# Alternating halves of the matmul array: 64-row score products and 64-wide value products in pairs

## The chip, the core and the metric

The kernel runs on one core of one Trainium2 chip. TensorE does the matmuls, VectorE, ScalarE and GpSimd the rest, and the queue on SyncE starts every load. The metric is the device time of one execution in microseconds, shown as the median of the runs.

## What is computed

One layer of a decoder in float32, 256 tokens of width 1024: a combined input projection, two attention branches of 8 heads each, gates, an output projection, and a sparse expert network (top 4 of 32 experts). Cut to the parts that matter here:

```
z = h @ W_in
A: multi-head latent attention: s = q_nope.k_nope + q_rot.k_rot (64 + 32 wide), causal softmax, p @ v (a v of 64 for each head)
B: sparse attention: index scores relu(q_idx . k_idx) of 8 heads, 64 wide, weighted and summed, top 64 keys of each query;
   s = q . k (64 wide, one k for all heads), softmax over the chosen keys, p @ v (one v of 64 for all heads)
x = x + W_out(sigmoid(g_A) * (A @ W_bA) + sigmoid(g_B) * (B @ W_bB))
x = x + experts(x), 12 MB of float32 weights for each of the 32 experts
```

## The kernel before

All work is written out by hand for each engine, with semaphores between the engines; an engine runs its instructions in the order of the code. The program has a front (everything up to the router) and a stage of 32 expert items. The expert weights come in units of 2 MB into a ring of twelve slots; a slot is loaded again when TensorE has read it (semaphore `used`).

Tokens are two tiles `t` of 128. A query tile t = 0 sees 128 keys, t = 1 sees 256. `BATCHES` lists six batches of head products that fill one PSUM bank of 512 columns: four heads for t = 0, two heads for t = 1. It is used three times:

- **index stage**: `scores` (L568) for b = 0 to 5 with the index q and k, in banks `SB[0]` and `SB[1]` in turn; ScalarE takes the relu of each batch (L987), VectorE adds it to the scores. One block of the gate projection (`gate_block`, L526, 8 matmuls of 256 columns) stands behind b = 3. Then `turn_pairs` transposes the q of branch B (L530).
- **attention loop**, iterations b = 0 to 11 on TensorE: scores of batch b + 1 (`scores_of`), values of batch b - 1 (`values`, L705), a gate block (b = 0 to 10), and the four transposes of the probabilities of batch b (`turn_probs`, L530). Batches 0 to 5 are branch A (96 rows), 6 to 11 branch B (`kT`, `qT`, 64 rows).
- For each batch VectorE masks the scores and finds the row maximum (`masked(b + 1)`), ScalarE takes the exponentials, VectorE divides by the sum (`normalised(b)`) and goes on with a piece of the top-k search for branch B; ScalarE copies the transposed probabilities to `probT` (L1051), which `values(b)` waits for (semaphore `pT_ok`).

The operands decide which part of the 128 x 128 array a matmul uses. In branch B and in the index stage head h has its 64 rows of q and k in partitions 0 to 63 (h even) or 64 to 127 (h odd), so its score product takes the upper or the lower half of the rows. A value product has 64 columns, and its output goes to partitions 0 to 63 (h even) or 64 to 127 (h odd), the left or the right half of the columns. The batches of before hold heads of one parity each, so the products of a batch all use the same half. A float32 matmul of the program is two rows "MATMUL" in the trace, called passes below.

The loop of TensorE before:

```python
            for b in range(12):
                if b < 11:
                    scores_of(b + 1)
                if b:
                    values(b - 1)
                if b in GATES_ATT:
                    gate_block()
                turn_probs(b)
```

Of the kernel before, what the change touches and what calls it, by code (L numbers as in the profile page):

```python
# [14 lines left out]
P = 128  # L15
# [42 lines left out]
BATCHES = [(0, (0, 2, 4, 6)), (0, (1, 3, 5, 7)),  # L58
           (1, (0, 2)), (1, (1, 3)), (1, (4, 6)), (1, (5, 7))]
# [5 lines left out]
GATES_IDX = (3,)  # L65
# [24 lines left out]
def build(nc, x, positions, attn_norm_g, w_in, mla_q_norm_g, mla_w_uq, mla_kv_norm_g, mla_w_ukv,  # L90
# [4 lines left out]
    with ctx:  # L95
# [106 lines left out]
        TURN = TB + SB  # L202
        ACC, GU, PREP, DN = B[0:4], B[4:6], B[6], B[7]
# [319 lines left out]
        def _(pe):  # L523
# [40 lines left out]
            def scores(b, q, k, signal):  # L564
                t, heads = BATCHES[b % 6]
                w = P * (t + 1)
                for m, h in enumerate(heads):
                    mm = pe.matmul(SB[b % 2][:, m * w:(m + 1) * w], q(h, t), k(h, w), start=True, stop=True)  # L568
                mm.then_inc(signal, 1)

            def pair_q(h, t):
                return qT[HD * (h % 2):HD * (h % 2) + HD, h // 2, t * P:(t + 1) * P]

            def pair_k(h, w):
                return kT[HD * (h % 2):HD * (h % 2) + HD, 0:w]
# [103 lines left out]
            def scores_of(b):  # L679
                if b >= 2:  # L680
                    pe.wait_ge(s_mx, b - 1)
                if b < 6:
                    scores(b, lambda h, t: qmT[:, h, t * P:(t + 1) * P], lambda h, w: kmT[:, h, 0:w], s_ps)
                else:
                    scores(b, pair_q, pair_k, s_ps)

            def turn_probs(b):
# [3 lines left out]
                for m in range(4):  # L691
                    tr = turned(TB[b % 2][:, m * P:(m + 1) * P], prob[:, b % 2, m * P:(m + 1) * P])
                tr.then_inc(pT_ps, 1)

            def values(b):
                t, heads = BATCHES[b % 6]
                pe.wait_ge(pT_ok, b + 1)
                if b in (6, 8):
                    pe.wait_ge(pv_ok, t + 1)
                for m in range(4):  # L700
                    h = heads[m // (t + 1)]
                    kt = m % (t + 1)
                    half = V_DIM * (h % 2)
                    v = v_ml[:, kt, h, :] if b < 6 else z_kv[:, kt, HD:2 * HD]
                    mm = pe.matmul(VB[t][half:half + V_DIM, (h // 2) * P:(h // 2 + 1) * P], v,  # L705
# [846 lines left out]
```

## Time and profile before

| | |
|---|---|
| median of 3 runs | 1149.29 us (1148.4 to 1149.75) |
| time of the profiled execution | 1149.92 us |
| its span, first to last instruction | 1148.1 us |
| mean granted TensorE clock | 0.993 of full speed |
| HBM read | 429.92 MB |

The time is 1.8 us more than the span of the same execution, and the profiled execution is 0.6 us above the median.

### The profile page before, as it was taken

The numbers are of one execution on the slowest core, as the hardware profiler recorded it, in microseconds if no ns is written. First come the engines' busy times: TensorE is split into PE (matmuls) and PEld (weight loads), VectorE is DVE, ScalarE is ACT, GpSimd is POOL, SyncE is SP. The second block draws the span as 40 slices with busy tenths as digits, with TensorE's granted clock in tenths as the row PEclk, the third lists the DMA queues.
The fourth block names the chain that finished last, engine by engine and source line by source line (L and its number), as shares of the span: only waits on it lengthen the run. The fifth ranks groups of instructions, "written<-read, shape, count | busy, mean of one in ns | idle before, by whom it ended". The sixth has DMA issues, their size and how long they took to land.

```text
span 1148.1 us, 13190 instructions
## 1 busy us (share of the span) xinstructions
PE 1100.0 (96%) x5094; PEld 478.2 (42%) x5094; DVE 279.3 (24%) x663; ACT 164.0 (14%) x341; POOL 10.2 (1%) x28
## 2 busy tenths in 40 slices
PE   7999999999999999999999999999999999999996
PEld 5578878553333333333333333333333333333332
DVE  2056533121222222222222222211111111112223
ACT  2144431211111010000011001000000000000002
POOL 0101000000000000000000000000000000000000
PEclk9999999998999999999999999999999999999999
DMA  9823541968999999999999999999999999999994
GB/s 316 324 74 147 220 200 56 369 263 350 432 432 430 431 432 433 430 430 432 432 432 430 430 432 433 430 431 431 433 432 430 430 433 433 430 431 432 433 431 196
DMA packets 43411, 431.23 MB, mean 376 GB/s; under 512 B 5825, under 2 KB 8257, under 8 KB 18785
## 3 DMA queue, kind: packets, MB, share of 16 engines
q1 hardware_dynamic: 43392, 430.99, 89.3%
q8 instruction: 12, 0.20, 0.1%
q14 instruction: 7, 0.05, 0.0%
HBM read 429.92 MB, written 1.05 MB: 375 GB/s over the span
## 4 chain that ended last, share of the span: by engine, by line
PE 65%; DMA 22%; SPq 10%; issue 1%; DVE 1%; ACT 1%; another core or an unknown queue 0%; DVEq 0%; ACTq 0%
PE bank L865 24%; DMA raw<-in_w_gate_up 21%; PE bank L881 12%; PE bank L526 8%; SPq L436 7%; PE bank L530 5%; PE bank L559 4%; PE bank L804 3%; SPq L439 3%; PE bank L837 3%; PE bank L751 2%; PE bank L568 1%; PE bank L705 1%; PE bank L769 1%; DMA x_res<-in_x 0%
## 5 line engine op out<-in xcount | busy, mean ns | idle before, releaser
L865 PE MATMUL bank<-raw,xT 128*64 128x512 f32 x2048 | 463.9, 599 | 27.3 <-DMA raw<-in_w_gate_up 25.9
L865 PEld LDWEIGHTS bank<-raw,xT 128*64 128x64 f32 x2048 | 140.1, 137 | 322.8 <-issue 258.3
L881 PE MATMUL bank<-raw,actT 128*64 128x512 f32 x1024 | 232.3, 595 | 0.0
L1440 DVE COPY ev_gu<-bank 128x512 f32<-128x512 f32 x32 | 22.1, 692 | 499.8 <-PE bank L865 499.8
L881 PEld LDWEIGHTS bank<-raw,actT 128*64 128x64 f32 x1024 | 70.8, 137 | 131.8 <-issue 124.7
L1433 DVE TENSOR_TENSOR gub<-bank,bias_gu 128x512 f32<-128x512 f32 x64 | 43.9, 686 | 169.5 <-PE bank L530 169.5
L1100 ACT COPY ev_gu<-bank 128x512 f32<-128x512 f32 x32 | 18.8, 586 | 392.7 <-PE bank L865 392.7
L837 PE MATMUL bank<-ev,gated 64*128 64x512 f32 x256 | 63.6, 615 | 1.2 <-ACT ev L1110 0.8
L804 PE MATMUL bank<-x_res,onehot 128*64 128x512 f32 x264 | 62.3, 592 | 0.0
L526 PE MATMUL bank<-hT,front_raw 128*128 128x256 f32 x256 | 58.9, 383 | 0.0
L526 PEld LDWEIGHTS bank<-hT,front_raw 128*128 128x128 f32 x256 | 47.5, 190 | 8.4 <-issue 2.5
L559 PE MATMUL bank<-front_raw,hT 128*128 128x512 f32 (+2 forms) x128 | 47.0, 531 | 1.1 <-DVE hT L1172 1.1
L530 PEld LDWEIGHTS bank<-cst,ev_gu 128*128 128x128 f32 x256 | 33.4, 210 | 25.9 <-issue 25.9
L1105 ACT ACTIVATE ev_gu<-gub 128x512 f32<-128x512 f32 x32 | 20.2, 630 | 154.7 <-DVE gub L1442 154.7
L530 PE MATMUL bank<-cst,ev_gu 128*128 128x128 f32 x256 | 39.7, 298 | 0.0
L837 PEld LDWEIGHTS bank<-ev,gated 64*128 64x128 f32 x256 | 22.1, 186 | 41.7 <-issue 41.0
L804 PEld LDWEIGHTS bank<-x_res,onehot 128*64 128x64 f32 x264 | 18.9, 137 | 37.2 <-issue 37.1
L559 PEld LDWEIGHTS bank<-front_raw,hT 128*128 128x128 f32 x128 | 25.7, 207 | 20.6 <-issue 20.5
L1110 ACT COPY ev<-bank 128x512 f32<-128x512 f32 x32 | 18.8, 586 | 82.9 <-PE bank L881 82.9
L1084 ACT COPY ev<-bank 128x512 f32<-128x512 f32 x33 | 19.3, 586 | 66.5 <-PE bank L804 66.5
L1093 ACT COPY gated<-bank 128x256 f32<-128x256 f32 x32 | 11.9, 372 | 113.4 <-PE bank L530 113.4
L1456 DVE TENSOR_TENSOR actT<-gub,ev_gu 128x512 f32<-128x512 f32 x32 | 22.2, 693 | 24.4 <-PE bank L881 24.3
(235 smaller groups left out, 599.5 us busy)
## 6 DMA issues: line engine op xcount, KB each, us to landing
raw<-in_w_gate_up SPq DMA_DIRECT2D x128, 2048.0 KB, 43.0
raw<-in_w_down SPq DMA_DIRECT2D x64, 2048.0 KB, 45.9
front_raw<-in_w_in SPq DMA_DIRECT2D x6, 2048.0 KB, 12.9
front_raw<-in_w_out SPq DMA_DIRECT2D x2, 2048.0 KB, 9.6
front_raw<-in_w_branch_mla SPq DMA_DIRECT2D x1, 2048.0 KB, 7.7
front_raw<-in_w_branch_dsa SPq DMA_DIRECT2D x1, 2048.0 KB, 7.7
front_raw<-in_w_in SPq DMA_DIRECT2D x1, 1664.0 KB, 16.3
x_res<-in_x SPq DMA_DIRECT2D x2, 512.0 KB, 4.4
```

What stands on the lines that cost most here:

```text
L436: sp.dma_start(raw[:, slot, :], w_gu_v[e, u // 2, :, u % 2 * UNIT:(u % 2 + 1) * UNIT]).then_inc(raw_in[slot], 16)
L439: sp.dma_start(raw[:, slot, :], w_dn_v[e, u]).then_inc(raw_in[slot], 16)
L526: mm = pe.matmul(o, lhs(c), rhs(c), start=start and c == 0, stop=c == n - 1)
L530: return pe.transpose(o, src, ident)
L559: mm = pe.matmul(ZB[t][:, 0:w], hT[:, c, t * P:(t + 1) * P], unit3(n, w)[:, c, :], start=c == 0, stop=c == KC - 1)
L751: mm = pe.matmul(B[2 * t + n][:, :], mT[:, c, t * P:(t + 1) * P], unit3(U_WO + n)[:, c, :], start=c == 0, stop=c == KC - 1)
L804: mm = pe.matmul(PREP[half * SLOTS:(half + 1) * SLOTS, :], onehot[:, t, :], xs[:, t, half * BLK:(half + 1) * BLK], start=t == 0, stop=t == ...
L837: mm = pe.matmul(ACC[2 * t + half][:, :], scat[rows, t * P:(t + 1) * P], ev[rows, :], start=False, stop=True, skip_group_check=True)
L865: mm = pe.matmul(GU[pair][half * SLOTS:(half + 1) * SLOTS, :], xT[:, c, b, :], w[:, at:at + BLK], start=u == 0 and k == 0, stop=last and k ...
L881: mm = pe.matmul(DN[half * SLOTS:(half + 1) * SLOTS, :], actT[:, c, u, :], w[:, at:at + BLK], start=u == 0 and c == 0, stop=u == DN_UNITS ...
L1433: dve.tensor_tensor(gub[:, pair, :].rearrange("p (j s) -> p j s", s=SLOTS), GU[pair][:, :].rearrange("p (j s) -> p j s", s=SLOTS), bias_gu ...
L1456: dve.tensor_tensor(actT[:, :, :, :].rearrange("p c h s -> p (c h s)"), lin, sig, ALU.mult).then_inc(act_ok, 1)
```

## The change

`BATCHES` now pairs the heads as (0, 1, 2, 3), (4, 5, 6, 7) and (0, 1), (2, 3), (4, 5), (6, 7), and is used for branch A alone, where the values of a batch now alternate between the column halves. `PAIR_BATCHES` is the old list, and serves the index stage and branch B. There two batches, one of even and one of odd heads, are issued together: `pair_scores` alternates between the row halves and writes two banks, `pair_values` multiplies the one v with all heads of a batch in one matmul (512 or 2 x 256 columns) and alternates between the column halves. VectorE and ScalarE do the same work as before; in the index stage batches 2 and 3 lie in other banks. The core of the diff:

```diff
-BATCHES = [(0, (0, 2, 4, 6)), (0, (1, 3, 5, 7)),
-           (1, (0, 2)), (1, (1, 3)), (1, (4, 6)), (1, (5, 7))]
+BATCHES = [(0, (0, 1, 2, 3)), (0, (4, 5, 6, 7)),
+           (1, (0, 1)), (1, (2, 3)), (1, (4, 5)), (1, (6, 7))]
+PAIR_BATCHES = [(0, (0, 2, 4, 6)), (0, (1, 3, 5, 7)),
+                (1, (0, 2)), (1, (1, 3)), (1, (4, 6)), (1, (5, 7))]
-GATES_IDX = (3,)
+GATES_IDX = (2,)
+        IDX_BANKS = (SB, TB, SB)
+            def pair_scores(b, banks, signal):
+                t = PAIR_BATCHES[b][0]
+                w, n = P * (t + 1), len(PAIR_BATCHES[b][1])
+                for m in range(n):
+                    for k in range(2):
+                        h = PAIR_BATCHES[b + k][1][m]
+                        rows = slice(HD * k, HD * k + HD)
+                        mm = pe.matmul(banks[k][:, m * w:(m + 1) * w], qT[rows, h // 2, t * P:(t + 1) * P], kT[rows, 0:w],
+                                       start=True, stop=True)
+                        if m == n - 1:
+                            mm.then_inc(signal, 1)
-            for b in range(6):
-                if b >= 2:
-                    pe.wait_ge(idx_rl, b - 1)
-                scores(b, pair_q, pair_k, idx_ps)
+            for b in range(0, 6, 2):
+                if b == 4:
+                    pe.wait_ge(idx_rl, 2)
+                pair_scores(b, IDX_BANKS[b // 2], idx_ps)
                 if b in GATES_IDX:
                     gate_block()
             pe.wait_ge(qb_rot, 1)
+            pe.wait_ge(idx_rl, 4)
             turn_pairs(z_qb, qd_ps)
...
                 else:
-                    scores(b, pair_q, pair_k, s_ps)
+                    pe.wait_ge(s_mx, b)
+                    pair_scores(b - 6, SB, s_ps)
...
+            def pair_values(b):
+                t, heads = PAIR_BATCHES[b - 6]
+                pe.wait_ge(pT_ok, b + 2)
+                pe.wait_ge(pv_ok, t + 1)
+                n = len(heads) * P
+                at = (heads[0] // 2) * P
+                for kt in range(t + 1):
+                    for k in range(2):
+                        mm = pe.matmul(VB[t][V_DIM * k:V_DIM * (k + 1), at:at + n], z_kv[:, kt, HD:2 * HD],
+                                       probT[:, (b + k) % 2, kt * n:(kt + 1) * n], start=kt == 0, stop=kt == t)
+                        if kt == t:
+                            mm.then_inc(pv_ps, 1)
...
-                if b < 11:
+                if b < 6 or b in (7, 9):
                     scores_of(b + 1)
-                if b:
+                if 0 < b < 7:
                     values(b - 1)
+                elif b in (8, 10):
+                    pair_values(b - 2)
...
-            values(11)
+            pair_values(10)
```

TensorE in the index stage, from the first index scores to the transposes of the next q (banks 4 and 5 are `SB`, 2 and 3 are `TB`, L526/L531 is the gate block, xN counts matmuls). Before:

```order
L568 MATMUL bank4<-kT,qT 128x128 x4
L568 MATMUL bank5<-kT,qT 128x128 x4
L568 MATMUL bank4<-kT,qT 128x256 x2
L568 MATMUL bank5<-kT,qT 128x256 x2
L526 MATMUL bank0<-hT,front_raw 128x256 x8
L568 MATMUL bank4<-kT,qT 128x256 x2
L568 MATMUL bank5<-kT,qT 128x256 x2
L530 MATMUL bank2<-cst,z_qb 128x128 x4
```

And of the change, the end of the same stretch, from the last scores of 128 columns on:

```order
L585 MATMUL bank5<-kT,qT 128x128
L585 MATMUL bank2<-kT,qT 128x256
...
L585 MATMUL bank3<-kT,qT 128x256
L531 MATMUL bank0<-hT,front_raw 128x256 x8
L585 MATMUL bank4<-kT,qT 128x256
L585 MATMUL bank5<-kT,qT 128x256
```

The matmuls are as many as before, but two of one bank no longer follow each other, and batches 2 and 3 stand in banks that no relu of batches 0 and 1 has to free.

TensorE in branch B, iterations 7 and 8 of the attention loop (`area_p` is `prob` or `probT`, `sq` holds v). Before:

```order
L568 MATMUL bank4<-kT,qT 128x256 [waits s_mx]
L568 MATMUL bank4<-kT,qT 128x256
L705 MATMUL bank6<-area_p,sq 64x128 [waits pv_ok,pT_ok]
L705 MATMUL bank6<-area_p,sq 64x128 x3
L526 MATMUL bank0<-hT,front_raw 128x256 [waits g_ok,raw_in2]
L526 MATMUL bank0<-hT,front_raw 128x256 x7
L530 MATMUL bank3<-cst,area_p 128x128 [waits pT_ok,p_ok]
L530 MATMUL bank3<-cst,area_p 128x128 x3
L568 MATMUL bank5<-kT,qT 128x256 [waits s_mx]
L568 MATMUL bank5<-kT,qT 128x256
L705 MATMUL bank6<-area_p,sq 64x128 [waits pT_ok]
```

And in the change:

```order
L585 MATMUL bank<-kT,qT 128x256 [waits s_mx]
L585 MATMUL bank<-kT,qT 128x256 x3
L531 MATMUL bank<-hT,front_raw 128x256 [waits g_ok,raw_in2]
L531 MATMUL bank<-hT,front_raw 128x256 x7
L535 MATMUL bank<-cst,area_p 128x128 [waits pT_ok,p_ok]
L535 MATMUL bank<-cst,area_p 128x128 x3
L731 MATMUL bank<-area_p,sq 64x512 [waits pv_ok,pT_ok]
L731 MATMUL bank<-area_p,sq 64x512
```

Scores of two batches stand together in the odd iterations, values of two batches in the even ones, where they now come straight behind the transposes that their `pT_ok` rests on; before, scores stood between the two.

## Rows read from the trace of the kernel before

**Rows 1.** Stretches: busy us of each engine with instructions, TensorE clock, DMA share, GB/s

```profile
240.00:245.00 5.00, 4.31 (x26) 2.37 (x26) 1.14 (x3) 0.59 (x1) 0.00 (x0) 1.00 0.00 0
...
270.00:275.00 5.00, 5.00 (x26) 1.85 (x24) 0.00 (x0) 0.00 (x0) 0.00 (x0) 1.00 0.58 190
280.00:690.00 410.00, 410.00 (x1942) 148.41 (x1940) 89.51 (x185) 43.21 (x78) 0.00 (x0) 1.00 1.01 431
690.00:1148.00 458.00, 421.53 (x1954) 146.36 (x1950) 95.73 (x200) 47.42 (x87) 0.00 (x0) 0.99 0.97 417
```

**Rows 2.** Timeline of TensorE, index stage: start, us, passes (x), idle before

```profile
61.94 3.52 PE L568 MATMUL bank<-kT,qT 64*128 64x128 f32 x24
65.39 3.72 PE L526 MATMUL bank<-hT,front_raw 128*128 128x256 f32 x16
69.04 1.14 PE L568 MATMUL bank<-kT,qT 64*128 64x256 f32 x8
70.11 1.09 PE L530 MATMUL bank<-cst,z_qb 128*128 128x128 f32 x8
```

**Rows 3.** Timeline of ScalarE, relu of index batch 3

```profile
66.85 0.60 ACT L987 ACTIVATE area_p<-bank 128x512 f32<-128x512 f32 x1 [0.95 <-DVE score L1221]
```

**Rows 4.** Timeline of TensorE, values in branch A

```profile
105.75 1.09 PE L705 MATMUL bank<-area_p,v_ml 128*64 128x128 f32 x8
106.77 3.72 PE L526 MATMUL bank<-hT,front_raw 128*128 128x256 f32 x16
```

**Rows 5.** Timeline of VectorE and TensorE, up to `turn_probs(3)`

```profile
100.00 0.69 DVE L1300 SCALAR_TENSOR_TENSOR area_p<-bank,cst 128x512 f32<-128x512 f32 x1 [1.27 <-PE bank L568]
...
121.25 0.69 DVE L1311 TENSOR_TENSOR area_p<-area_p,den 128x512 f32<-128x512 f32 x1
...
122.27 0.60 PE L530 MATMUL bank<-cst,area_p 128*128 128x128 f32 x4
```

**Rows 6.** Timeline of TensorE, branch B, iterations 6 and 7

```profile
134.43 0.60 PE L530 MATMUL bank<-cst,area_p 128*128 128x128 f32 x4
...
137.06 3.72 PE L526 MATMUL bank<-hT,front_raw 128*128 128x256 f32 x16
140.62 0.60 PE L530 MATMUL bank<-cst,area_p 128*128 128x128 f32 x4
141.15 1.13 PE L568 MATMUL bank<-kT,qT 64*128 64x256 f32 x4
142.21 1.09 PE L705 MATMUL bank<-area_p,sq 128*64 128x128 f32 x8
143.22 3.72 PE L526 MATMUL bank<-hT,front_raw 128*128 128x256 f32 x16
```

**Rows 7.** Timeline of VectorE, branch B, iteration 7

```profile
142.31 0.69 DVE L1295 SCALAR_TENSOR_TENSOR area_p<-bank,allow 128x512 f32<-128x512 f32 x1 [3.74 <-PE bank L568]
```

**Rows 8.** Timeline of TensorE, iteration 11 and the end of the loop

```profile
165.27 0.60 PE L530 MATMUL bank<-cst,area_p 128*128 128x128 f32 x4
166.54 1.09 PE L705 MATMUL bank<-area_p,sq 128*64 128x128 f32 x8 [0.67 <-ACT area_p L1051]
167.56 0.66 PE L530 MATMUL bank<-cst,area_p 128*128 128x128 f32 x4
168.05 1.89 PE L526 MATMUL bank<-mlaT,front_raw 128*128 128x256 f32 x8
```

**Rows 9.** Timeline of TensorE, expert stage: products alternating between column halves

```profile
282.89 3.62 PE L881 MATMUL bank<-raw,actT 128*64 128x512 f32 x16
286.43 1.23 PE L530 MATMUL bank<-cst,ev_gu 128*128 128x128 f32 x8
```

**Rows 10.** Stretch of the lower TensorE clock, columns as in Rows 1

```profile
262.60:269.50 6.90, 5.47 (x18) 2.44 (x18) 4.59 (x9) 0.63 (x1) 0.00 (x0) 0.51 0.72 306
```

**Rows 11.** Timeline of TensorE, gate and up products of expert items 0 and 1

```profile
242.51 13.95 PE L865 MATMUL bank<-raw,xT 128*64 128x512 f32 x64
...
265.50 15.86 PE L865 MATMUL bank<-raw,xT 128*64 128x512 f32 x64 [1.43 <-DVE xT L1424]
```

More of the change, by code:

```diff
@@ L562, in z_unit, with scores @@
                     z_n += 1
-            def scores(b, q, k, signal):
-                t, heads = BATCHES[b % 6]
+            def scores(b):
+                t, heads = BATCHES[b]
                 w = P * (t + 1)
                 for m, h in enumerate(heads):
[L568 to L575, printed above, removed]
+                    mm = pe.matmul(SB[b % 2][:, m * w:(m + 1) * w], qmT[:, h, t * P:(t + 1) * P], kmT[:, h, 0:w],
+                                   start=True, stop=True)
+                mm.then_inc(s_ps, 1)
+            def pair_scores(b, banks, signal):
[6 more added lines that the diff above has]
+                        mm = pe.matmul(banks[k][:, m * w:(m + 1) * w], qT[rows, h // 2, t * P:(t + 1) * P], kT[rows, 0:w],
+                                       start=True, stop=True)
+                        if m == n - 1:
+                            mm.then_inc(signal, 1)
             def turn_pairs(zq, signal):
@@ L682, in scores_of @@
                 if b < 6:
-                    scores(b, lambda h, t: qmT[:, h, t * P:(t + 1) * P], lambda h, w: kmT[:, h, 0:w], s_ps)
+                    scores(b)
                 else:
-                    scores(b, pair_q, pair_k, s_ps)
+                    pe.wait_ge(s_mx, b)
+                    pair_scores(b - 6, SB, s_ps)
             def turn_probs(b):
@@ L691, in turn_probs @@
                 for m in range(4):
-                    tr = turned(TB[b % 2][:, m * P:(m + 1) * P], prob[:, b % 2, m * P:(m + 1) * P])
+                    at = (m % 2) * 2 + m // 2 if b >= 8 else m
+                    tr = turned(TB[b % 2][:, at * P:(at + 1) * P], prob[:, b % 2, m * P:(m + 1) * P])
                 tr.then_inc(pT_ps, 1)
             def values(b):
-                t, heads = BATCHES[b % 6]
+                t, heads = BATCHES[b]
                 pe.wait_ge(pT_ok, b + 1)
[L698 to L705, printed above, removed]
-                                   probT[:, b % 2, m * P:(m + 1) * P], start=kt == 0, stop=kt == t)
-                mm.then_inc(pv_ps, 1)
+                for kt in range(t + 1):
+                    for n, h in enumerate(heads):
+                        m = n * (t + 1) + kt
+                        half = V_DIM * (h % 2)
+                        mm = pe.matmul(VB[t][half:half + V_DIM, (h // 2) * P:(h // 2 + 1) * P], v_ml[:, kt, h, :],
+                                       probT[:, b % 2, m * P:(m + 1) * P], start=kt == 0, stop=kt == t)
+                mm.then_inc(pv_ps, 1)
+            def pair_values(b):
[4 more added lines that the diff above has]
+                at = (heads[0] // 2) * P
+                for kt in range(t + 1):
+                    for k in range(2):
[3 more added lines that the diff above has]
+                            mm.then_inc(pv_ps, 1)
             pe.wait_ge(up_d, 4)
@@ L1212, in _ @@
             for b in range(6):
-                t, heads = BATCHES[b]
+                t, heads = PAIR_BATCHES[b]
                 w = P * (t + 1)
```

10 lines of the change are left out of this document (5 added, 5 removed).

## The prediction

> **What bounds the kernel now.** I read the stretches first, to learn which part of the program a gain can come out of. The program has two regimes. In the middle and late part the DMA engines are full: share 1.01 at 431 GB/s from 280 us on [rows 1], with TensorE busy all 410 us up to 690, and 421.53 of 458 us after that, when it waits for weights. So in the expert stage the weight stream sets the pace in the end. But the stream does not start by itself. It stands still at 240 to 245 us (DMA share 0.00) and is at 0.58 at 270 to 275 us [rows 1], because all twelve slots of the ring are full and only TensorE's reading frees one. From about 273 us on it never stops again. The end is therefore that moment plus the bytes that are left: what TensorE saves before its first expert products moves the whole stream, and with it the end, one to one. What it would save after 280 us would be worth nothing, and the change touches nothing there.
>
> Then the front, by the timeline of TensorE. In branch B the rows follow each other without an idle time [rows 6], and VectorE idles 3.74 us there for the next scores [rows 7]: TensorE is the bound. The one exception is in branch A. VectorE starts the first mask at 100.00 us and has, with its pieces of the top-k search, next to no gap until the division of batch 3 ends at 121.25 + 0.69 = 121.94 us; `turn_probs(3)` comes at 122.27 [rows 5]. There TensorE is only 0.33 us behind the point where VectorE would hold it.
>
> **What a pass costs.** The gate block: 16 passes of 256 columns from 137.06 to 140.62, 0.22 us each with the change of shape [rows 6]; so about 0.108 us for 128 columns, 0.43 for 512. The values of before: 8 passes of 128 columns, all in one column half, from 105.75 to 106.77 [rows 4]: 1.02 us, that is 8 x 0.108 and 0.15 for the change of shape. Half an array is no faster than a whole one, if only one half is used.
>
> **Do the halves run side by side?** For the row halves the trace already shows it. Index batches 4 and 5, one even and one odd, wait for nothing between them: 8 passes of 256 columns from 69.04 to 70.11 [rows 2], 1.07 us. A single batch of 4 such passes takes 1.06 us (141.15 to 142.21) [rows 6]. Two batches at the price of one. For the column halves the trace shows it at 512 columns: the down products alternate, and 16 passes take 282.89 to 286.43 [rows 9], 3.54 us or 0.22 a pass, where one half alone would need 0.43. At 128 and 256 columns it isn't shown. Its bounds are nothing gained (8 passes 1.02 us) and half the passes' time (0.15 + 4 x 0.108 = 0.58, say 0.60). I take 0.60, by the 512-column row. A pair of value batches in branch B is 0.15 + 2 x 0.43, or 0.15 + 4 x 0.216: 1.0 us for both, where it was 2.04; with nothing gained it stays at 2.0.
>
> The Trainium skill speaks against the column half of this: TensorE: Matmul & The Clock Gate, "Part 3: Packing small matmuls — row/col tiling", says that a weight load overlaps with matmuls under way only where the row group differs, and column halves share their row groups. By it the value batches would keep their price; the third case below has that sum. The down products, with a new weight load at each pass, do not bear it out at 512 columns.
>
> **Index stage.** Before, 61.94 to 65.39 for batches 0 to 3: 3.45 us, with a wait for the relu of batch 0. Now 8 passes per half of 128 columns and 4 of 256, 0.87 + 0.87 + 0.2 = 1.94: saved 1.5. Batches 4 and 5 already overlap: 0. The transposes after them now need the relu of batch 3, as they write its bank; it ends at 66.85 + 0.60 = 67.45 [rows 3], and they would start at 70.11 - 1.5 = 68.6. Covered. ScalarE and VectorE reach their next work from batch 4's scores, so they shift with TensorE. Sum: **1.5 us**.
>
> **Attention loop**, by what stands between two gate blocks (the blocks themselves stay at 3.56 us). The new cost is a wait: where no scores stand between transposes and values, TensorE must wait for ScalarE's copy. Before this happened once, in iteration 11: transposes at 165.27, values at 166.54 [rows 8], 1.27 us instead of the 0.53 from 140.62 to 141.15 [rows 6]. It now happens in iterations 6, 8 and 10, and behind it are queued the gate block and all that follows.
> - Iterations 1 to 3: 3 x 0.42 saved on values, but VectorE holds `turn_probs(3)` at 121.94 + 0.06 = 122.0. Only 0.27 is left of 1.26. What is late next is nothing: VectorE then idles.
> - Iterations 4 and 5: values 0.42 each, 0.84. The double scores in 5 cost what one batch did.
> - Iteration 6: 134.43 to 137.06, 2.63 [rows 6]; now 1.27 + 0.60. Saved 0.76.
> - Iterations 7 and 9: 140.62 to 143.22, 2.60; now 0.53 + 1.07 = 1.60. Saved 2 x 1.00.
> - Iterations 8 and 10: 2.60; now 1.27 + 1.0 = 2.27. Saved 2 x 0.33.
> - Iteration 11: 165.27 to 168.05, 2.78 [rows 8]; now two groups of transposes, 0.43 + 0.53 = 0.96, if the division of batch 11 is done by then: its scores now come an iteration earlier, so yes. Saved 1.8.
> - `pair_values(10)` takes 1.0 like `values(11)`. It waits for the second copy of the transposes, but `branch(0, 0)`, 8 passes or 1.83 us, stands before it. 0.
>
> Sum: 0.27 + 0.84 + 0.76 + 2.0 + 0.66 + 1.8 = 6.3 us. An iteration is at least 0.53 + 1.07 + 3.56 = 5.2 us long, and VectorE's work in it without top-k, now free to begin at the transposes in every second one, is 6.16 (the iteration) - 3.74 = 2.4 us; ScalarE comes between. So neither becomes the bound in branch B.
>
> Total 1.5 + 6.3 = **7.8 us**. Against the profiled execution: 1149.92 - 7.8 = 1142.1. Its time is 0.6 above the median, so I give 1149.29 - 7.8 = 1141.5.
>
> **Rivals.**
> 1. *As worked out*, 0.70. Its own range is 1139.8 to 1143.4, of which the clock is the larger part. At 262.6 to 269.5 us TensorE was granted 0.51, its level of 1.2 GHz, after it had been busy only in part [rows 10]; the same 64 passes took 15.86 us at item 1 and 13.95 at item 0 [rows 11], 1.9 us. The change shifts what TensorE does against that, and the 1.9 can go or double.
> 2. *The gain is larger*, 0.04: the low clock is missed, and the copy is waited for less. 1138.5 to 1139.8.
> 3. *Column halves do not overlap at short passes*, 0.13. For it: only 512 columns are shown. Against it: nothing in the row at 512 hints at a load that isn't hidden. Then turn_probs(3) and iterations 4, 5: 0; 6: 2.63 - 1.27 - 1.02 = 0.34; 7 and 9: 2.0; 8 and 10: 2 x (2.60 - 1.27 - 2.0) = -1.34; 11: 1.8; `pair_values(10)`: -1.0. Sum 1.8, with the index 3.3: 1146.0.
> 4. *The chain through the softmax eats part*, 0.05: VectorE, ScalarE and the copies become the pace in iterations 8 to 11, half of the 4.5 us there is lost: 1143.8.
> 5. *The gain isn't passed on*, 0.04: 1149.3. It would need a weight stream with a start of its own, and the share of 0.00 at 240 us [rows 1] speaks against it.
> 6. *Slower*, 0.04: the new gaps (1.0 us before `turn_probs(3)`, 0.7 us each in iterations 6, 8, 10) bring TensorE to 1.2 GHz in the loop. At that level about a half of a stretch's time is lost (1.9 of 4 to 7 us), so it decides from some 16 us of loop at the low level on; with the whole loop there, 60 us of work at about double, the time would be far above 1160, with 20 us of it 1152. Against it: gaps of 0.67 us at 166.5 are there before and the granted clock stays at 1.00 through the loop.
>
> **How the numbers follow.** The time is that of case 1, 1141.5. The range 1139.6 to 1146.2 holds cases 1, 4 and the middle of 3, and leaves out 2, 5, 6 and what lies beyond 3: under 0.2. About 0.2% (2.3 us) is what a measurement can tell here; cases 1 to 4 are faster by more than that: 0.92; case 5 the same, 0.04; case 6 slower, 0.04.
>
> **What the profile after would show.** Index scores of batches 0 to 3 in one stretch of about 1.9 us, not 3.45. Values in branch A 0.6 us from start to start of the gate block; if 1.0, case 3. The double values about 1.0 us (2.0 in case 3). An idle time of TensorE before `turn_probs(3)` of about 1 us with VectorE's division as its releaser, and three of 0.7 us before values, released by ScalarE. Gate blocks 5.2 us apart in iterations 7 and 9. The weight stream saturated from about 265 instead of 273 us, its rate still 431 GB/s. The prediction is wrong if the gate blocks are closer but that start hasn't moved, if the granted clock in the loop leaves 1.00, or if the double values take 2 us.

## The result and the profile after

The changed kernel takes 1138.55 us (median of 6 runs, 1137.58 to 1140.71). The kernel before, measured beside it, takes 1148.92 us (6 runs, 1147.55 to 1149.75). The ratio is 0.9914, with a 95% interval of 0.9903 to 0.9925: 10.4 us faster, where 7.8 were forecast. The predicted 1141.5 us is 3 us too high, and the measured median lies 1.05 us below the lower end of the range.

The profiled execution of after takes 1137.86 us, with a span of 1136.1 us (1148.1 before). Its page is almost that of before:

```profile
PE 1085.6 (96%) x5066; PEld 466.2 (41%) x5066; DVE 279.3 (25%) x663; ACT 163.5 (14%) x341; POOL 10.2 (1%) x28
```

VectorE and ScalarE do the same work as before; TensorE has a span that is 12 us shorter. The page does not say where. The timeline of TensorE does, read at the same places as before. First the index stage (start, us, engine, line, operation, tiles, passes):

```profile
60.80 2.03 PE L585 MATMUL bank<-kT,qT 64*128 64x128 f32 x24
62.76 3.72 PE L531 MATMUL bank<-hT,front_raw 128*128 128x256 f32 x16
66.41 1.13 PE L585 MATMUL bank<-kT,qT 64*128 64x256 f32 x8
67.47 1.09 PE L535 MATMUL bank<-cst,z_qb 128*128 128x128 f32 x8
```

From the first scores to the gate block are 1.96 us, where [rows 2] had 3.45. From the first scores to the transposes of the next q are 6.67 us in all, where they were 8.17: 1.5 saved. The values of branch A, in which the column half now alternates at 128 columns:

```profile
103.11 0.66 PE L718 MATMUL bank<-area_p,v_ml 128*64 128x128 f32 x8
103.70 3.72 PE L531 MATMUL bank<-hT,front_raw 128*128 128x256 f32 x16
```

Eight passes take 0.59 us from start to start, against 1.02 in [rows 4]. `turn_probs(3)`, by the timelines of TensorE and, below it, of VectorE:

```profile
119.36 0.65 PE L535 MATMUL bank<-cst,area_p 128*128 128x128 f32 x4 [0.86 <-DVE area_p L1340]
```

```profile
118.62 0.69 DVE L1340 TENSOR_TENSOR area_p<-area_p,den 128x512 f32<-128x512 f32 x1
```

The division ends at 119.31 and TensorE goes on at 119.36: VectorE is the bound at this one place, and TensorE idles 0.86 us. Then branch B, iterations 6 to 11 and the values behind the loop:

```profile
130.73 0.60 PE L535 MATMUL bank<-cst,area_p 128*128 128x128 f32 x4
132.00 0.66 PE L718 MATMUL bank<-area_p,v_ml 128*64 128x128 f32 x8 [0.67 <-ACT area_p L1080]
132.59 3.72 PE L531 MATMUL bank<-hT,front_raw 128*128 128x256 f32 x16
136.15 0.60 PE L535 MATMUL bank<-cst,area_p 128*128 128x128 f32 x4
136.68 1.14 PE L585 MATMUL bank<-kT,qT 64*128 64x256 f32 x8
137.74 3.72 PE L531 MATMUL bank<-hT,front_raw 128*128 128x256 f32 x16
141.30 0.60 PE L535 MATMUL bank<-cst,area_p 128*128 128x128 f32 x4
142.57 1.08 PE L731 MATMUL bank<-area_p,sq 128*64 128x512 f32 x4 [0.67 <-ACT area_p L1080]
143.58 3.72 PE L531 MATMUL bank<-hT,front_raw 128*128 128x256 f32 x16
...
152.29 0.60 PE L535 MATMUL bank<-cst,area_p 128*128 128x128 f32 x4
153.57 1.08 PE L731 MATMUL bank<-area_p,sq 128*64 128x256 f32 x8 [0.68 <-ACT area_p L1080]
154.58 3.72 PE L531 MATMUL bank<-hT,front_raw 128*128 128x256 f32 x16
158.14 1.04 PE L535 MATMUL bank<-cst,area_p 128*128 128x128 f32 x8
159.01 1.89 PE L531 MATMUL bank<-mlaT,front_raw 128*128 128x256 f32 x8
160.83 1.08 PE L731 MATMUL bank<-area_p,sq 128*64 128x256 f32 x8
```

The reader is to see three things. Between two gate blocks lie 1.59 us (136.15 to 137.74) in iteration 7 and 2.28 in iteration 8, where [rows 6] had 2.60. The double values take 1.01 us, at 512 columns and at 256. And the copy of ScalarE is waited for three times, 0.67 or 0.68 us each. The loop starts at 96.20 and ends at 159.01, 62.81 us; before it was 98.84 to 168.05 ([rows 8] has the end), 69.2.

The start of the saturated stream, by stretches (columns as in [rows 1]):

```profile
255.00:260.00 5.00, 4.68 (x22) 1.96 (x24) 2.48 (x6) 0.00 (x0) 0.00 (x0) 1.00 0.40 167
260.00:265.00 5.00, 5.00 (x26) 2.07 (x24) 0.00 (x0) 0.00 (x0) 0.00 (x0) 1.00 0.98 367
275.00:690.00 415.00, 415.00 (x1961) 149.64 (x1962) 91.81 (x191) 42.97 (x78) 0.00 (x0) 1.00 1.01 431
690.00:1136.00 446.00, 409.44 (x1900) 142.40 (x1896) 92.71 (x192) 46.43 (x85) 0.00 (x0) 1.00 0.97 416
```

The share is 0.98 from 260 us on, where before it was still 0.58 at 270 to 275; the rate is the same. The first down product of item 1 stands at 270.80, and 1136.1 - 270.8 = 865.3 us follow; before, 1148.1 - 282.89 = 865.2 ([rows 9]). All of the 12 us is won ahead of it.

But the stages give 1.5 + 6.4 = 7.9 us. The rest is neither in the index stage nor in the loop. The router, by TensorE's timeline, before and then after (ten small products of constants, 20 passes, whose result is not used):

```profile
231.62 4.11 PE L769 MATMUL bank<-cst 128*128 128x128 f32 x20
```

```profile
222.57 2.48 PE L798 MATMUL bank<-cst 128*128 128x128 f32 x20
```

The same instructions cost 1.63 us more before. The granted clock there, by stretches, before:

```profile
231.80:235.20 3.40, 3.40 (x17) 3.40 (x17) 2.79 (x15) 0.32 (x1) 0.00 (x0) 0.50 0.77 236
```

And the first gate and up products of item 1, with the stretch ahead of them (columns as in [rows 1]) and then by TensorE's timeline, after:

```profile
251.00:254.40 3.40, 2.90 (x13) 2.44 (x12) 1.59 (x3) 0.63 (x1) 0.00 (x0) 0.50 0.97 414
```

```profile
251.06 1.98 PE L535 MATMUL bank<-cst,ev_gu 128*128 128x128 f32 x8
...
255.32 13.95 PE L894 MATMUL bank<-raw,xT 128*64 128x512 f32 x64 [1.43 <-DVE xT L1453]
```

The products take 13.95 us, where [rows 11] has 15.86 at the same place: the stretch at 1.2 GHz of [rows 10], which was 6.8 us long and reached into them, has become one of 3.4 us (251.0 to 254.4) that ends before them, and costs only the transposes there (1.98 us for 8 passes). In sum: 1.1 us from an earlier first index product (61.94 to 60.80, where the program is still the same), 1.5, 6.4, 1.6 in the router, 1.9 at item 1, less 0.5 for the transposes: 12.0.

### The profile page after: what moved, and what is told of

The parts are those of the page before. It is cut to its first block, busy times and chain, and to the rows that moved or that the text cites. A ratio compares the mean times of both kernels' runs of the same rounds, so it can differ in the third digit from the quotient of the medians.

```text
span 1136.1 us, 13139 instructions
## 1 busy us (share of the span) xinstructions
PE 1085.6 (96%) x5066; PEld 466.2 (41%) x5066; DVE 279.3 (25%) x663; ACT 163.5 (14%) x341; POOL 10.2 (1%) x28
## 3 DMA queue, kind: packets, MB, share of 16 engines
HBM read 429.92 MB, written 1.05 MB: 379 GB/s over the span
## 4 chain that ended last, share of the span: by engine, by line
PE 63%; DMA 22%; SPq 11%; DVE 2%; issue 1%; ACT 1%; another core or an unknown queue 0%; DVEq 0%; ACTq 0%
PE bank L894 24%; DMA raw<-in_w_gate_up 22%; PE bank L910 12%; PE bank L531 7%; SPq L441 7%; PE bank L535 5%; PE bank L564 4%; PE bank L833 3%; SPq L444 3%; PE bank L866 3%; PE bank L780 2%; PE bank L585 1%; PE bank L798 0%; DMA x_res<-in_x 0%; PE bank L876 0%
## 5 line engine op out<-in xcount | busy, mean ns | idle before, releaser
L833 PE MATMUL bank<-x_res,onehot 128*64 128x512 f32 x264 | 62.3, 592 | 0.0
L531 PE MATMUL bank<-hT,front_raw 128*128 128x256 f32 x256 | 58.9, 383 | 0.0
L531 PEld LDWEIGHTS bank<-hT,front_raw 128*128 128x128 f32 x256 | 47.5, 190 | 9.5 <-issue 3.7
```

Source lines behind the costliest of these rows:

```text
L531: mm = pe.matmul(o, lhs(c), rhs(c), start=start and c == 0, stop=c == n - 1)
L833: mm = pe.matmul(PREP[half * SLOTS:(half + 1) * SLOTS, :], onehot[:, t, :], xs[:, t, half * BLK:(half + 1) * BLK], start=t == 0, stop=t == ...
```

## The experiments

All times are medians, with the kernel before measured beside; "stage" numbers are read from TensorE's timeline as above. Two questions were put. First, which part of the change gives what, and whether the overlap of the halves is its mechanism. Second, where the 1.5 to 2.5 us beyond the 7.9 come from: theory A, chance of the clock at places behind the change and of the start-up; theory B, something of the change that the stages don't show. (The expectation of `index_only` calls them theory 1 and theory 2.)

**One part alone.** `index_only` keeps `pair_scores` in the index stage and takes the rest back, `values_a_only` keeps only the new `BATCHES` in branch A, `branch_b_only_2` only the pairs of branch B:

```diff
# index_only, against the kernel before (a part)
-            for b in range(6):
-                if b >= 2:
-                    pe.wait_ge(idx_rl, b - 1)
-                scores(b, pair_q, pair_k, idx_ps)
+            for b in range(0, 6, 2):
+                if b == 4:
+                    pe.wait_ge(idx_rl, 2)
+                pair_scores(b, IDX_BANKS[b // 2], idx_ps)
...
# values_a_only, against the kernel before (a part)
-BATCHES = [(0, (0, 2, 4, 6)), (0, (1, 3, 5, 7)),
-           (1, (0, 2)), (1, (1, 3)), (1, (4, 6)), (1, (5, 7))]
+BATCHES = [(0, (0, 1, 2, 3)), (0, (4, 5, 6, 7)),
+           (1, (0, 1)), (1, (2, 3)), (1, (4, 5)), (1, (6, 7))]
...
# branch_b_only_2, against the changed kernel (a part; its index stage is put back as well)
-BATCHES = [(0, (0, 1, 2, 3)), (0, (4, 5, 6, 7)),
-           (1, (0, 1)), (1, (2, 3)), (1, (4, 5)), (1, (6, 7))]
+BATCHES = [(0, (0, 2, 4, 6)), (0, (1, 3, 5, 7)),
+           (1, (0, 2)), (1, (1, 3)), (1, (4, 6)), (1, (5, 7))]
...
```

> Only the index stage is changed (pairs of batches, batches 2 and 3 in other banks, gate block behind batch 2), the attention loop is that of before. Theory 1 (what the rows of the two traces show as local savings is all that is certain, and the rest of the 10.4 us came from where TensorE's clock was low in those executions): about 1.5 us less than before, ratio 0.9987. Theory 2 (a systematic gain of 2 to 3 us comes with the front being earlier at all, whatever made it earlier): 3 to 4 us less, ratio 0.9970.

> Only the heads of branch A are paired so that its value products alternate between the column halves; index stage and branch B as before. If column halves overlap at 128 columns: a group of value passes 0.60 us instead of 1.02, and 1.5 us less in all (6 x 0.42, of which VectorE takes 1.0 back before turn_probs(3)), ratio 0.9987. If the rule on weight loads held: 0.

> Only branch B is changed (double scores and double values, with the new waits for the copy); index stage and branch A as before. By the rows: 0.34 + 2.0 + 0.66 + 1.8 = 4.8 us between the first scores and the first branch product (69.2 before), so 64.4. Time 1144 if nothing else moves.

Measured: `index_only` 1145.55 us, ratio 0.9975 (0.9966 to 0.9984), index stage 6.67 us, loop 69.21. `values_a_only` 1145.89 us, 0.9977 (0.9967 to 0.9987), index stage 8.18, loop 67.70. `branch_b_only_2` 1143.11 us, 0.9955 (0.994 to 0.997), 8.18 and 64.31. The savings in the stages are 1.51, 1.52 and 4.91 us, 7.94 together, and the whole change saves 7.9: they add up. The times themselves fall by more, 2.9, 2.6 and 5.2 us by the ratios. For `index_only` the 0.9987 of theory 1 lies outside the interval, and the 0.9970 of theory 2 in it; for `values_a_only` the 0.9987 lies at its edge. So two of the parts alone already bring something that their stages do not show; the table below and what follows it come back to this. In `values_a_only` VectorE holds `turn_probs(3)` as in the whole change:

```profile
120.86 0.66 PE L533 MATMUL bank<-cst,area_p 128*128 128x128 f32 x4 [0.85 <-DVE area_p L1314]
```

**The order of the halves.** `together_not_alternating` does all passes of one half, then all of the other; nothing else changes:

```diff
-                for m in range(n):
-                    for k in range(2):
+                for k in range(2):
+                    for m in range(n):
```

(and the same two loops in `pair_values`).

> The changed kernel, but within a pair of batches all matmuls of one half are issued first, then all of the other half (scores and values); branch A keeps its alternation. If TensorE starts passes strictly in order, the second half waits for the first: every double group takes about twice as long, some 1 us more at each of 3 index groups, 3 score groups and 3 value groups, about 9 us slower than the changed kernel. If it looks ahead past matmuls whose half is busy, as index batches 4 and 5 of before suggest (8 passes of 256 columns in 1.07 us), groups of 4 passes per half cost the same as alternating, those of 8 passes per half some 0.4 us more: within 1.5 us of the changed kernel, 1140.

Measured: 1141.35 us, ratio 0.9935 (0.9918 to 0.9951). The index stage takes 7.23 us instead of 6.67, the loop 63.36 instead of 62.81. The scores of batches 6 and 7, 16 passes of 128 columns, there:

```profile
126.19 1.71 PE L585 MATMUL bank<-kT,qT 64*128 64x128 f32 x16
127.83 0.66 PE L718 MATMUL bank<-area_p,v_ml 128*64 128x128 f32 x8
```

And in the changed kernel:

```profile
125.49 1.16 PE L585 MATMUL bank<-kT,qT 64*128 64x128 f32 x16
126.58 0.66 PE L718 MATMUL bank<-area_p,v_ml 128*64 128x128 f32 x8
```

1.64 us against 1.09. One half after the other without any overlap would be 0.15 + 16 x 0.108 = 1.88. So the order is worth 0.55 at eight passes a half, in each of two places, and part of the overlap is there even so: TensorE does not hold a pass of the idle half back until the other half's passes are through. At four passes a half (the pairs of 256 columns) the order makes no difference, 1.07 us in both kernels.

The same run divides the gain of the index stage. Its batches stand there in the same order as in the kernel before, and only their banks differ; yet it takes 7.23 us and not 8.18. The weight loads of TensorE, before and then in `together_not_alternating`, show what is gone:

```profile
61.94 1.52 PEld L568 LDWEIGHTS bank<-kT,qT 64*128 64x128 f32 x16 [0.60 <-issue]
63.78 1.28 PEld L568 LDWEIGHTS bank<-kT,qT 64*128 64x128 f32 x8 [0.32 <-ACT area_p L987]
```

```profile
60.96 2.17 PEld L585 LDWEIGHTS bank<-kT,qT 64*128 64x128 f32 x24 [0.60 <-issue]
```

Before, batch 2 waits for the relu that frees its bank; with banks of their own batches 2 and 3 don't. In all, of the 7.9 us some 0.95 come from the banks of the index stage, 1.5 from the alternation in the values of branch A (which this run keeps), 1.1 from the alternation in the pairs, and the other 4.4 from pairs of batches in branch B standing next to each other, less what the new waits cost.

**The new waits taken away.** The 0.67 us before values in iterations 6, 8 and 10 is a matter of order alone. `values_late` puts these values behind the gate block, and `values_late_topk_split` also lets VectorE break off its top-k search once more, before the division that `turn_probs(3)` waits for:

```diff
-                if 0 < b < 7:
+                if 0 < b < 6:
                     values(b - 1)
-                elif b in (8, 10):
-                    pair_values(b - 2)
                 if b in GATES_ATT:
                     gate_block()
+                if b == 6:
+                    values(b - 1)
+                elif b in (8, 10):
+                    pair_values(b - 2)
# only in values_late_topk_split
-                        if r % 3 == 2:
+                        if r % 3 == 2 or (t == 1 and r == TOPK // 8 - 1):
                             yield
```

> The changed kernel with the values of iterations 6, 8 and 10 behind the gate block instead of ahead of it. Theory: the three new idle times of 0.67 us before values are a plain loss that the gate block can cover. It expects the attention loop 2.0 to 2.2 us shorter than the 62.81 us of the changed kernel, about 60.7, and the time 2 us below it. Rival: VectorE's and ScalarE's chain for the next division becomes the wait instead, and the loop stays at 62.8.

> As values_late, and the last piece of the top-k search (7.0 us of VectorE in iteration 2 with the mask and the division) is split in two, so that its second half runs in iteration 3. Theory: turn_probs(3) no longer waits for VectorE (0.86 us idle and some 0.2 us of load in the changed kernel), the loop is 1.0 us shorter than in values_late, about 59.7. Rival: VectorE is late one iteration further on, and nothing is gained.

Measured: 1137.39 us, ratio 0.9904 (0.9889 to 0.992), loop 60.44 us; and 1136.21 us, 0.9901 (0.9886 to 0.9916), loop 59.36. The three waits were worth 2.37 us, the one for VectorE 1.08. Iteration 8 of the second kernel has no idle time left:

```profile
139.51 0.60 PE L535 MATMUL bank<-cst,area_p 128*128 128x128 f32 x4
139.95 3.62 PE L531 MATMUL bank<-hT,front_raw 128*128 128x256 f32 x16
143.50 1.08 PE L731 MATMUL bank<-area_p,sq 128*64 128x512 f32 x4
144.51 0.66 PE L535 MATMUL bank<-cst,area_p 128*128 128x128 f32 x4
```

Both are a little more than forecast (2.0 to 2.2, and 1.0). The 2.37 are more than 3 x 0.67 = 2.0; a part of the rest is that a gate block starts 0.44 us behind the first transpose (139.51 to 139.95), where scores start 0.53 behind it. `all_three` is `values_late_topk_split` with the halves one after the other:

> values_late_topk_split with the products of a pair put one half after the other, as in together_not_alternating. Index stage 6.67 + 0.56 = 7.23 us, loop 59.36 + 0.55 = 59.9 or less, since part of the products' time now lies in front of waits for ScalarE's copies. Together 1.1 us later than values_late_topk_split: 1136.2 + 1.1 = 1137.3, 1135.5 to 1138.5 with what the clock gives or takes. If the pairs of halves were not overlapping at all in either order, nothing would change in the stages.

Measured: 1138.22 us, ratio 0.9906 (0.9885 to 0.9928), index stage 7.23, loop 59.93. The stages are as forecast to 0.03 us; the time is 0.9 above the 1137.3, within the range given.

**The same two kernels once more.** For the second question both were run again under other labels, with no edit.

> The changed kernel once more, on the chip and beside the runs of the next three. If what it gains beyond the 7.9 us of its own stretches is chance of where TensorE's clock was low, its distance to the kernel before here lies between 6 and 12 us and differs from the 10.4 of the first comparison, with index stage 6.67 us and attention loop 62.8 us again. If it is systematic, the distance is 10.4 again.

> The kernel before once more. Index stage 8.18 us and attention loop 69.2 us again; its low stretches, and so the time from the first branch product to the end, may stand elsewhere than in its first profile (74.46 us to the first expert product, with one in the router). In theory 1 it comes out without the one in the router about as often as with it.

Measured: 1139.01 us (1135.49 to 1140.58), ratio 0.9917 (0.9896 to 0.9938), and 1148.30 us, ratio 0.9993 (0.998 to 1.0007). The kernel before, run beside both, has a median of 1149.36 us: the distance of the medians is 10.35 us once more, which is what was expected of a systematic gain, but the interval reaches from 7 to 12 us and does not exclude 7.9. The index stage and the loop are 6.67 and 62.82, 8.18 and 69.23. But this time the changed kernel is at the lower clock in the router, and in a longer stretch at item 1:

```profile
221.47 3.81 PE L798 MATMUL bank<-cst 128*128 128x128 f32 x20
...
255.46 15.40 PE L894 MATMUL bank<-raw,xT 128*64 128x512 f32 x64 [1.43 <-DVE xT L1453]
```

So that the 1.63 us in the router and most of the 1.9 us at item 1 were missing in the first profile is no property of the changed kernel.

**Everything later by a known amount.** Small products of constants (9, or 14) ahead of the first attention scores, in the kernel before and in the changed one:

```diff
+            for _ in range(9):
+                pe.matmul(VB[1][:, 0:P], const("ones"), ident, start=True, stop=True)
             scores_of(0)
```

> The kernel of before with 9 more small matmuls (18 passes of 128 columns, 1.96 us) on TensorE ahead of the first attention scores; their result is not used. Theory 1 (the stretches at 1.2 GHz fall where they fall, whatever the start of the expert stage): 1.96 us more than before, 1150.6. Theory 3 (the stretches stand where they do because of when TensorE gets to the router, so that any shift of the front can add or remove some 2 us): it differs from before by clearly other than 2.0 us, and the profile has no low stretch in the router or another one between the first two expert items.

> The changed kernel with nine products of constants ahead of the first attention scores, 1.96 us by the same nine in the kernel before. If what comes early on TensorE moves the end one to one: 1138.9 + 2.0 = 1140.9 (1140.2 to 1141.6). If the time at which TensorE reaches the router and the items sets its clock there, it can come out up to 2 us above or below that.

> The kernel before with fourteen such products, 3.05 us. One to one: 1148.3 + 3.05 = 1151.3 (1150.7 to 1152.0). If the place in time sets the clock, off that by up to 2 us; if VectorE's mask is the bound there instead, less than 1149.3.

Measured: `before_plus_2us` 1149.59 us, ratio 1.0015 (1.0004 to 1.0025); `after_plus_2us` 1139.97, 0.9919 (0.9907 to 0.9932); `before_plus_3us` 1150.69, 1.0015 (1.0006 to 1.0023). In the timeline the products cost 2.1 us (nine, with the change of shape) and 3.2 us (fourteen), and the span without the clock's part (table below) grows by as much. Two of the three forecasts missed: 1139.97 lies below 1140.2 to 1141.6, and 1150.69 just below 1150.7 to 1152.0. The 1150.6 for `before_plus_2us` is 1.0 us too high, though its distance is as forecast. The medians grow by less: `before_plus_2us` by 1.9 us of 2.1 (1147.70 beside it), `before_plus_3us` by 2.0 of 3.2 (1148.67), and `after_plus_2us` by 1.2 of 2.1, against 1138.8, the mean of the changed kernel's two medians. The profile of `after_plus_2us` has no stretch of the lower clock at the router or at item 1; both of the changed kernel have one at item 1. In the profiles what comes late is passed on to the end in full; in two of the three medians about 1 us of it is missing.

**The idle time at item 1 filled.** `gap_filled_*` puts 7 products of constants where TensorE waits 1.43 us for VectorE ahead of item 1, `both_filled_*` puts 4, 4 and 6 around the transposes there and 5 ahead of the second router product, each in both kernels. The edit of `gap_filled_*`:

```diff
             turn(0)
             turn_tokens(1)
+            for _ in range(7):
+                pe.matmul(DN[:, 0:P], ones, ident, start=True, stop=True)
```

> The kernel before with 7 small matmuls (14 passes of 128 columns, 1.5 us) in the 1.43 us in which TensorE waits for the tokens of expert item 1. If that idle time is what leads to the low stretch there (1.9 us lost in the up products of item 1), item 1's products take 13.95 us in the profile and the time is 1 to 2 us below before. Rival: the fill starts later than the idle and pushes the products back: up to 0.3 us slower; the low stretch comes all the same.

> The same fill in the changed kernel. With the low stretch between the items gone in both kernels, their distance comes nearer to the 7.9 us that the index stage and the loop give: 7 to 9 us. If more than that is systematic it stays above 10.

> The kernel before, with small products of constants (128 columns, into a bank that is not read) put where TensorE waits: four and four and six around the transposes between items 0 and 1 of the experts, five more ahead of the second router product. If the 1.5 to 2 us beyond the stage savings come from the low clock at these two places, this runs at about 1147 (1.6 us less now and then in the router, 1.9 at the item), and no stretch below 1.00 is left there. If the clock is low there whatever TensorE does, it stays at 1148.5.

> The same products in the changed kernel. Theory A (the stages save 7.9, the rest is the clock at these two places): 1139.1, the distance to both_filled_before is 7.9, 7.2 to 8.6. Theory B (something in the change saves 9 to 10 us that the stages do not show): the distance stays at 9.0 to 10.

Measured: `gap_filled_before` 1147.89 us, ratio 0.9992 (0.9981 to 1.0003), `gap_filled_after` 1139.22, 0.992 (0.9903 to 0.9938). Their medians are 8.7 us apart, in the forecast 7 to 9. The profile of `gap_filled_before` has no lower clock at item 1, but neither has `before_plus_3us`, in which nothing was filled; and `gap_filled_after` has it, from 251.9 us on, ahead of the filled wait. So the fill is not shown to take it away. `both_filled_before` 1149.90, 1.0014 (1.0005 to 1.0023), `both_filled_after` 1141.61, 0.9938 (0.9925 to 0.9951). These missed: the fill of `both_filled` costs 1.69 us in the item gap, so neither absolute time came out as forecast. `both_filled_before` has full clock at both places (1.00 from 240.8 to 281.0) and a stretch at 1126 us instead; in the changed kernel the lower clock stays. In the timeline of `both_filled_after`, the first products of the fill:

```profile
251.20 1.91 PE L935 MATMUL bank<-cst 128*128 128x128 f32 x8
```

Eight passes at 1.91 us, although TensorE had been busy without a gap since the first products of item 0. Nor does the distance of the two, 8.3 us, part 7.9 from 9 to 10: the two ratios leave it open by 1.8 us.

**What settles the profiled executions.** The span of each of the 18 profiles, less the start of its first index product, less what the lower clock added to four parts of it: to the way from the first branch product to item 0 (72.83 us at full clock), from there to item 1 (22.46), to the first down product (15.47), and behind it (865.2). In the two `both_filled` rows 1.69 us of fill are taken off as well.

| kernel | start | index | loop | clock added | rest |
|---|---|---|---|---|---|
| before | 61.9 | 8.18 | 69.22 | 4.1 | 1082.1 |
| before_again | 60.6 | 8.18 | 69.23 | 4.0 | 1082.0 |
| gap_filled_before | 60.6 | 8.18 | 69.22 | 3.3 | 1082.1 |
| both_filled_before | 61.9 | 8.18 | 69.21 | 1.7 | 1082.1 |
| index_only | 61.8 | 6.67 | 69.21 | 2.4 | 1080.6 |
| values_a_only | 60.8 | 8.18 | 67.70 | 2.4 | 1080.6 |
| branch_b_only_2 | 62.3 | 8.18 | 64.31 | 2.5 | 1077.0 |
| after | 60.8 | 6.67 | 62.81 | 1.0 | 1074.3 |
| after_again | 59.4 | 6.67 | 62.82 | 4.0 | 1074.1 |
| gap_filled_after | 61.7 | 6.67 | 62.83 | 1.4 | 1074.0 |
| both_filled_after | 60.9 | 6.67 | 62.82 | 3.0 | 1074.2 |
| together_not_alternating | 61.0 | 7.23 | 63.36 | 0 | 1075.3 |
| values_late | 60.9 | 6.67 | 60.44 | 1.6 | 1071.6 |
| values_late_topk_split | 60.9 | 6.67 | 59.36 | 1.6 | 1070.7 |
| all_three | 61.7 | 7.23 | 59.93 | 4.1 | 1071.8 |
| after_plus_2us | 62.1 | 6.67 | 62.74 | 0 | 1076.1 |
| before_plus_2us | 61.5 | 8.17 | 69.14 | 2.4 | 1084.2 |
| before_plus_3us | 61.6 | 8.18 | 69.14 | 1.6 | 1085.1 |

The fifth column is what these four parts take beyond their time at full clock. That it is the clock is not assumed: a part up to the first down product in which the profile has no stretch at 1.2 GHz takes its time at full clock to 0.03 us in each profile that has no fill; the part behind it does so to 0.3 us, though all 18 have such a stretch in their last 8 us. The lower clock in the router adds 1.6 us in each of the eight profiles that have it. The last column is then the kernel: the four of before agree to 0.1 us, the four of the changed one to 0.3, and the distance is 7.9. Columns two and five differ between executions of one kernel by up to 1.4 and 3.0 us. Theory B falls for the profiled executions: there is nothing in them that the stages don't show.

The times over all runs have a surplus all the same. Before is 1148.4 us in the mean (113 runs made beside the others or again, 1143.6 to 1150.3) and the changed kernel 1138.9 (12 runs, 1135.5 to 1140.7): 9.5 us, give or take 0.9 (95%). The 1.6 beyond 7.9 are more than the chance of twelve runs. But most of it does not need the change. Put the mean of each kernel beside 1148.4 plus the difference of the last column, and most lie below that sum, also those in which nothing was made faster: `gap_filled_before` (mean 1147.5) by 0.9 us, `before_plus_2us` (1149.5) and `before_plus_3us` (1150.4) by about 1.0, as `index_only` (1145.7) by 1.2, `values_a_only` (1145.6) by 1.3 and the changed kernel by 1.6 (give or take 0.6 to 0.9 each). `both_filled_before` (0.3 above) and `all_three` (0.0) do not. So a front that comes later has a surplus too: it is less a gain of the others than something that the kernel before loses more often than most of them. The clock is the likely cause: the granted clock listed with each run is 0.9952 in the mean of the changed kernel's 12 runs and 0.9942 in 104 of before; 0.001 of 1140 us is 1.1 us, the most that this can be worth (an estimate). That is argued and not shown, as only one execution of each run has a trace, and the start-up of the others is not on record.

## Why the prediction missed

**The mechanism and its sum held.** Index stage 1.5 forecast, 1.5 measured. Attention loop 6.3 forecast, 6.4 measured. Its terms, by the rows above and by the same places of before:

- Iterations 1 to 3: 0.27 of 1.26 us, because VectorE holds `turn_probs(3)`. It stands 23.16 us after the loop's start, against 23.43 (122.27 in [rows 5], less 98.84): 0.27. The idle time of about 1 us is 0.86.
- Iterations 4 and 5: 0.84 forecast. From `turn_probs(3)` to the transposes of iteration 6 are 11.37 us, against 12.16: 0.79.
- Iteration 6: 0.76; measured 2.63 - 1.86 = 0.77.
- Iterations 7 and 9: 1.60 from transposes to gate block; measured 1.59.
- Iterations 8 and 10: 2.27; measured 2.28 and 2.29. The wait for the copy is 0.67 or 0.68, as in iteration 11 of before.
- Iteration 11: 1.8; measured 2.78 - 0.87 = 1.91. The branch products behind the transposes have their shape of tile, so the second group of transposes takes 0.44 to the next product as well, where 0.53 was put in, the time up to products of another shape.
- `pair_values(10)`: 1.02 us and no wait ahead of it. 0, as forecast.
- Passed on to the end: yes, 865.3 us behind the first down product against 865.2.

**Case 3, column halves that don't overlap at short passes, is wrong.** Eight passes take 0.59 us at 128 columns, and double values 1.01. The Trainium skill, TensorE: Matmul & The Clock Gate, "Part 3: Packing small matmuls — row/col tiling", lets a weight load overlap only where the row group differs. The measurement says that alternating column halves, each with a new load, run at the price of half the passes; it decides. The 8 passes of one column half in [rows 4] already bore on it: the profile of before counts as many weight loads as passes, and these passes take 8 x 0.108 us and the change of shape, half of what the passes of 256 columns take, so no load shows between them although the row group stays the same. Cases 4 to 6 did not happen: the granted clock stays at 1.00 in the loop, and no chain through the softmax appeared beside the one at `turn_probs(3)`.

**The step that failed is the clock term in case 1's own range**: "At 262.6 to 269.5 us TensorE was granted 0.51 [...] 1.9 us. The change shifts what TensorE does against that, and the 1.9 can go or double." The median is 2.95 us below the forecast: 0.4 because the kernel before, run beside, is that much below the 1149.29 taken, 0.1 from the stages, and 2.5 from what the stages do not show. Over all runs that last part is 1.6, and the mean of 1138.9 us is outside the range as well. Three things were wrong with the term.

First, its size. The trace of before had a second stretch of the lower clock, in the router at 231.8 to 235.2, that was not read, and that costs 1.63 us. Together the lower clock cost 4.1 us in the profiled execution of before, as much as in any of the 18 profiles, so that up to 4.1 us could go and next to nothing could come. Second, its condition, "after it had been busy only in part". TensorE's timeline of before:

```profile
242.51 13.95 PE L865 MATMUL bank<-raw,xT 128*64 128x512 f32 x64
256.30 1.89 PE L804 MATMUL bank<-x_res,onehot 128*64 128x512 f32 x8
258.11 3.70 PE L847 MATMUL bank<-bd,gateT 32*128 32x512 f32 x8
261.74 1.48 PE L530 MATMUL bank<-cst,ev_gu 128*128 128x128 f32 x8
263.01 1.06 PE L530 MATMUL bank<-cst,ev 128*128 128x128 f32 x4
```

TensorE has no idle time from 242.51 to 264.07, and the clock is low from 262.5 on: the 1.43 us of idle time of [rows 11] fall into the stretch and not ahead of it. Third, its cause: the term lets the change move the 1.9 us, but the stretches come and go between executions of one kernel, with 1.0 us in one of the changed kernel and 4.0 in the other. The start-up, which differs by up to 2.9 us between the 18 executions (59.4 to 62.3) in kernels that are the same up to there, was not in the range at all. With 4.1 us below the sum, the range would have reached 1137.4 and held the time; that is known only afterwards.

That the gain is 2.6 us larger than forecast was case 2 ("the low clock is missed"), which was given 0.04. Its first half is what the first profile of the changed kernel shows (1.0 us of it left, of 4.1 before), though not the second one (4.0); its other half, a shorter wait for the copy, is not true (0.67 us). Which of the unprofiled runs had which stretch stays open.

## What to carry to other kernels

Where products use half of TensorE's rows or columns, put the two halves' work next to each other; the price of a pair is then that of one, for short passes too, and at four passes a half the exact order within the pair no longer matters. Look also at what frees the banks: 0.95 us of the index stage's 1.5 was that. Where pairing leaves transposes, a copy on another engine and the products on it in a row, put a block of independent work between them: here that was worth another 2.4 us of the loop, and the version that also splits the top-k search is the fastest of the study, 1136.2 us. And before a sum gets a range, list every stretch of lower clock in the profile with its price: any of them can be gone in the next execution, and what they add differed from 1.0 to 4.0 us between two executions of one kernel, which is a third of what this change is worth. To tell whether a surplus belongs to a change, also move the old kernel by a known amount: here it showed the same surplus.

## What the runs showed of the hardware

- Column halves of the array run side by side at 128, 256 and 512 columns with a new weight load at each pass: 8 passes of 128 columns 0.59 us, against 1.02 in one half.
- Passes of one row half are not held back by waiting passes of the other, up to some distance: 8 and 8 passes of 128 columns in a row take 1.64 us, where 1.88 would be no overlap (an estimate, 0.15 + 16 x 0.108) and 1.09 is alternating; 4 and 4 of 256 columns take 1.07 either way.
- A stretch at 1.2 GHz can begin without any idle time of TensorE ahead of it: at 262.5 us in the kernel before, after 20 us without a gap, and at 251.4 in `both_filled_after` (1.91 us for eight passes), both behind products that use 64 columns or 32 rows of the array. It is there in one execution and gone in another of the same kernel, at 1.63 us a piece in the router.
